# A feed-forward block on one NeuronCore: seven half-size products in place of eight

## What is computed

```python
D_MODEL = 1024
D_FF = 4 * D_MODEL

def _rmsnorm(x, g):
    xf = x.astype(jnp.float32)
    y = xf * lax.rsqrt(jnp.mean(xf * xf, axis=-1, keepdims=True) + NORM_EPS)
    return (y * g.astype(jnp.float32)).astype(x.dtype)

def _mlp(h, w1, w2):
    a = jax.nn.relu(jnp.einsum('btd,df->btf', h, w1))
    return jnp.einsum('btf,fd->btd', a * a, w2)
```

## Time and profile before

| what | value |
|---|---|
| median of 3 runs | 2421.88 us (2419.75 to 2430.71) |
| the profiled execution, its own time | 2421.98 us |
| its span | 2420.4 us |
| PE busy | 2147.9 us, 89% of the span, 14280 matmuls |
| DVE, ACT, POOL busy | 36%, 29%, 14% |
| DMA | 154.45 MB, mean 64 GB/s |

### The profile page before, as it was taken

The page is one execution under the profiler, slowest core; times in us unless marked ns, Lnnn a source line. Parts: engine busy times, 40 slices in busy tenths (PEclk is TensorE's granted clock), DMA queues, the critical chain, the costliest instruction groups (busy, mean ns, idle before and its releaser), DMA issues. The chain is left out here.

```text
span 2420.4 us, 37774 instructions
## 1 busy us (share of the span) xinstructions
PE 2147.9 (89%) x14280; PEld 1437.8 (59%) x14280; DVE 863.1 (36%) x1637; ACT 701.1 (29%) x1285; POOL 330.9 (14%) x245
## 2 busy tenths in 40 slices
PE   4889966798998989989499969896999999999998
PEld 2445634576776667655366646564566666666666
DVE  4211141554544445454633444524222221221223
ACT  5112221343443434424333224312110110211212
POOL 4200022300000000000101111101430420510410
PEclk7998978899999999989799989997999999999999
DMA  6421442111111111131110024421111111111111
GB/s 210 115 69 49 149 122 66 53 46 37 54 36 55 36 37 54 37 84 35 28 44 9 21 98 138 136 107 35 52 47 49 50 46 52 44 51 52 43 35 72
DMA packets 191808, 154.45 MB, mean 64 GB/s; under 512 B 9200, under 2 KB 178310, under 8 KB 191370
## 3 DMA queue, kind: packets, MB, share of 16 engines
q1 hardware_dynamic: 182250, 140.01, 19.0%
q0 software_dynamic: 4640, 10.60, 1.6%
q10 hardware_dynamic: 4800, 2.30, 0.3%
HBM read 125.71 MB, written 31.33 MB: 65 GB/s over the span
## 5 line engine op out<-in xcount | busy, mean ns | idle before, releaser
L426 PE MATMUL ps<-hH,wH 128*128 128x352 f16 x1536 | 319.2, 317 | 47.7 <-ACTq L399 27.8
L426 PE MATMUL ps<-hL,wH 128*128 128x352 f16 x1536 | 318.0, 317 | 0.0
L426 PE MATMUL ps<-hH,wL 128*128 128x352 f16 x1536 | 317.2, 316 | 0.0
L413 DVE SCALAR_TENSOR_TENSOR wL<-w,wH 128x1024 f16<-128x1024 f32 x98 | 120.0, 1225 | 324.4 <-ACT wH L406 310.3
L426 PEld LDWEIGHTS ps<-hH,wH 128*128 128x128 f16 x1536 | 151.7, 99 | 134.0 <-issue 49.2
L426 PE MATMUL ps<-mH,wH 128*128 128x352 f16 x960 | 196.4, 314 | 9.5 <-DVEq L399 8.1
L426 PEld LDWEIGHTS ps<-hL,wH 128*128 128x128 f16 x1536 | 152.3, 99 | 82.4
L426 PEld LDWEIGHTS ps<-hH,wL 128*128 128x128 f16 x1536 | 151.8, 99 | 81.7
L426 PE MATMUL ps<-mL,wH 128*128 128x352 f16 x960 | 196.4, 314 | 0.0
L426 PE MATMUL ps<-mH,wL 128*128 128x352 f16 x960 | 196.0, 313 | 0.0
L1252 ACT COPY oL<-ps 128x512 f32<-128x512 f32 (+7 forms) x256 | 103.0, 402 | 297.2 <-PE ps L1211 297.2
(11 more groups left out here) (411 smaller groups left out, 2910.3 us busy)
## 6 DMA issues: line engine op xcount, KB each, us to landing
w<-in_mlp_w SPq DMA_DIRECT2D x64, 512.0 KB, 4.0
w<-in_w_in SPq DMA_DIRECT2D x32, 512.0 KB, 3.9
gw<-in_w_in SPq DMA_DIRECT2D x26, 512.0 KB, 4.7
gates<-cmpT SPq DMA_DIRECT2D x24, 528.0 KB, 3.0
mgsg<-gates SPq DMA_DIRECT2D x24, 528.0 KB, 4.3
mgw<-in_w_branch SPq DMA_DIRECT2D x24, 256.0 KB, 2.8
xTd<-xT SPq DMA_DIRECT2D x1, 4224.0 KB, 13.8
xT<-xTd SPq DMA_DIRECT2D x1, 4224.0 KB, 13.7
```

Source lines behind the costliest of these rows:

```text
L413: self.k.nc.vector.scalar_tensor_tensor(self.k.wL[:, slot % 2, :, :], self.k.w32[:, slot, :, :], WS, self.k.wH[:, slot % 2, :, :], ALU.mul ...
L426: ins = nc.tensor.matmul(k.ps[:, 3 * parity + c, 0:CH], w[:, kt, :], x[:, kt, c * CH:(c + 1) * CH], start=(kt == 0 and x is inH and w is w ...
```

## The change

`Dense` and `norm` are replaced for this block alone, by the class `Wino` and by `norm_wino`; `mlp` is rewritten. All other stages stay as they were.

The 1056 tokens are cut into two halves of 528 (`HT`), the contraction of 1024 into two halves of 512, and two weight tiles side by side form a pair, so that a pair is a 2 x 2 product of blocks. Instead of eight half-size products (128 x 512 by 512 x 528) it makes seven, P1 to P7, of sums and differences of blocks (Strassen's scheme, in the order `ORDER`). The four block sums of the weights are made by VectorE; `s1` holds one, three are written over `w32`. Those of the input are T1 to T4. Each product splits its own weight block into high and low, in a ring of four. It has 24 matmuls of 264 columns and a PSUM slot of two banks, four slots in rotation. There are 32 pairs, 224 products.

What comes out of PSUM is joined by more block sums. ScalarE copies P1 (`one`) and P5 (`five`) out, and VectorE takes out the other five with an addition. In the first layer GpSimd joins two blocks, VectorE squares the four blocks in place with the ReLU, and since the second layer needs T1 to T4 of the squared activations too, GpSimd subtracts those four. All seven operands (B11, B21, B22, T1 to T4) are then split: high parts on ScalarE, low parts of B on VectorE, low parts of T on GpSimd. In the second layer GpSimd makes the six additions to `xT` that the seven products need beside VectorE's. At the start of `mlp` the block sums T2, T3 and T4 of the norm's output are made and split, in instructions of 4 x 528 columns.

```diff
+HT = T // 2
+HC = HT // 2
+PAIRS = 2 * FF // (2 * P)
+GROUP = 2 * KD // 2
+ORDER = ('P1', 'P2', 'P6', 'P7', 'P4', 'P5', 'P3')
...
 def norm_wino(k, gcol, nxt):
...
+            for kt in range(KD):
+                nc.vector.scalar_tensor_tensor(cols3(nxt.x[kt // 4][:, kt % 4, :]), cols3(xT[:, kt, :]), k.vec[:, gcol + kt:gcol + kt + 1],
+                                               dense_out(k.ps, 0), ALU.mult, ALU.mult).then_inc(scaled, 1)
+            dve.wait_ge(scaled, KD)
+            tt(nxt.spare[0], nxt.x[0][:, :, HT:T], nxt.x[0][:, :, 0:HT], ALU.subtract)
...
         @block.tensor
         def _(pe):
+                pe.wait_ge(wn.lo, rel(PER, p + 1))
...
+                for kt in range(4):
+                    if n % GROUP == FIRST and kt in (0, 2, 3):
+                        made = n - FIRST + max(kt, 1)
+                        if u[0] == 'B':
+                            pe.wait_ge(b_lo, rel(3 * FIRST, b_at(made, u)))
+                        else:
+                            pe.wait_ge(t_lo, rel(4 * FIRST, t_at(made, u)))
+                    for w, x in ((wH, xH), (wH, xL), (wL, xH)):
+                        for c in range(2):
+                            ins = nc.tensor.matmul(k.ps[:, 2 * (p % 4) + c, 0:HC], w[:, kt, :], x[:, kt, c * HC:(c + 1) * HC],
...
         @block.scalar
         def _(act):
+            for p, (n, q) in enumerate(seq):
+                for u in H_BEFORE.get(p, ()):
+                    h_high(u)
+                if p + 3 < N:
+                    split(p + 3)
+                if first_layer(n) and q == 'P6':
+                    a_high(n, 'B11')
+                if first_layer(n) and q == 'P5':
+                    a_high(n, 'B21')
+                if n and first_layer(n - 1):
+                    for u in {'P1': ('T2',), 'P2': ('B22', 'T3'), 'P7': ('T4', 'T1')}.get(q, ()):
+                        a_high(n - 1, u)
+                if n > PAIRS - FIRST and q in ('P2', 'P6'):
+                    square_x(n - 1, ('P2', 'P6').index(q))
+                if q in ('P1', 'P5'):
+                    copy_out(p, n, q)
...
         @block.vector
         def _(dve):
+            sums(0, ('P5', 'P7', 'P6'))
+            tt(hx['T2'], hx['B22'], hx['T1'], ALU.subtract).then_inc(h_made, 1)
+            split(2)
+            h_low('T2')
+            sums(0, ('P3',))
+            for p, (n, q) in enumerate(seq):
+                for u in H_BEFORE.get(p, ()):
+                    h_low(u)
+                if p + 3 < N:
+                    split(p + 3)
+                if q == 'P5' and n + 1 < PAIRS:
+                    sums(n + 1, ('P5', 'P7', 'P6'))
+                elif q == 'P1' and n:
+                    sums(n, ('P3',))
...
+                if n and first_layer(n - 1) and q == 'P6':
+                    b_low(n - 1, 'B22')
+                if q in ('P2', 'P6', 'P7', 'P4', 'P3'):
+                    out(p, n, q)
+                if first_layer(n):
+                    for u in {'P2': ('B11',), 'P4': ('B21',), 'P3': ('B12', 'B22')}.get(q, ()):
+                        square(n, u)
+                    for u in {'P6': ('B11',), 'P5': ('B21',)}.get(q, ()):
+                        b_low(n, u)
...
         @block.gpsimd
         def _(pool):
+            tt(hx['T3'], hx['B22'], hx['B12'], ALU.subtract).then_inc(h_shared, 1)
+            pool.wait_ge(h_made, 1)
+            tt(hx['T4'], hx['B21'], hx['T2'], ALU.subtract).then_inc(h_shared, 1)
...
+                if not first_layer(n):
...
+                    x_add(n, '11+1', one)
...
+                    x_add(n, '12+2', c12)
...
+                    x_add(n, '21+3', c22)
+                    x_add(n, '22+3', c22)
...
+                    x_add(n, '12+5', five)
+                    x_add(n, '22+5', five)
+                    continue
+                pool.wait_ge(copied, copied_at(n, 'P5'))
+                pool.wait_ge(evac, evac_at(n, 'P4'))
+                tt(c12, c12, five, ALU.add).then_inc(joined, 1)
+                tt(c22, c22, five, ALU.add).then_inc(joined, 1)
+                pool.wait_ge(joined, joined_at(n, 'B22'))
+                pool.wait_ge(squared, squared_at(n, 'B12'))
+                tt(five, c12, c11, ALU.subtract).then_inc(t_made, 1)
+                pool.wait_ge(squared, squared_at(n, 'B22'))
+                pool.wait_ge(t_made, t_made_at(n, 'T1'))
+                tt(t2, c22, five, ALU.subtract).then_inc(t_made, 1)
+                tt(t3, c22, c12, ALU.subtract).then_inc(t_made, 1)
+                t_low(n, 'T2')
+                t_low(n, 'T3')
+                pool.wait_ge(b_lo, b_at(n, 'B21'))
+                tt(c21, c21, t2, ALU.subtract).then_inc(t_made, 1)
+                t_low(n, 'T4')
+                t_low(n, 'T1')
```

More of the change, by code:

```diff
@@ new lines, in norm_wino, with part @@
+def norm_wino(k, gcol, nxt):
+    nc, xT = k.nc, k.xT
+    summed, ms_ready, root_ready, step = k.sem("n2_summed"), k.sem("n2_ms"), k.sem("n2_root"), k.sem("n2_step")
+    diag_ready, spread, scaled, hi_ready = k.sem("n2_diag"), k.sem("n2_spread"), k.sem("n2_scaled"), k.sem("n2_hi")
+    NC = NT + 1
+    with nc.sbuf_tensor("n2dg", [P, NC, P], F32) as diag, nc.sbuf_tensor("n2st", [P, 4, 16], F32) as st, nc.Block() as block:
+        ms, root, y, t2 = (st[:, i, 0:NC] for i in range(4))
+        def part(kt):
+            u = 'B11' if kt < 4 else 'B21'
+            return nxt.x[kt // 4][:, kt % 4, 0:HT], nxt.h[u][0][:, kt % 4, :], nxt.h[u][1][:, kt % 4, :]
@@ L2248, in _ @@
         @block.sync
         def _(sp):
[L2250 to L2259, removed]
+            for n in range(2):
+                for i in range(2):
+                    nxt.load(sp, n, i)
@@ L2261, in _ @@
         @block.tensor
         def _(pe):
[L2263 to L2273, removed]
+            for t in range(NC):
+                w = P if t < NT else TS
+                ins = nc.tensor.matmul(k.ps[0:w, 7, t:t + 1], k.ssq[:, t * P:t * P + w], k.c('ones')[:, 0:1], start=True, stop=True)
@@ L2275, in _ @@
+            ins.then_inc(summed, 1)
+            pe.wait_ge(diag_ready, 1)
+            for c in range(3):
+                ins = nc.tensor.matmul(k.ps[:, c, 0:CH], k.c('ones'), diag[:, :, :].rearrange("p t n -> p (t n)")[:, c * CH:(c + 1) * CH],
+                                       start=True, stop=True)
+            ins.then_inc(spread, 1)
         @block.scalar
         def _(act):
[L2277 to L2286, removed]
@@ L2288, in _ @@
-            dn.split_hi(act, 0, 0, 0)
-            groups(act, tile)
+            act.wait_ge(ms_ready, 3)
+            nc.scalar.activation(root, ms, ACT.Sqrt).then_inc(root_ready, 1)
+            nxt.wait_tile(act, 0, 1)
+            for p in range(2):
+                nc.scalar.activation(nxt.ring(p)[0], nxt.quarter(0, 1, p + 1), ACT.Copy, scale=WS).then_inc(nxt.hi, 1)
+            for kt in range(KD):
+                x, hi, lo = part(kt)
+                act.wait_ge(scaled, kt + 1)
+                nc.scalar.copy(hi, x).then_inc(hi_ready, 1)
@@ L2291, in _ @@
         @block.vector
         def _(dve):
[L2293 to L2306, removed]
@@ new lines, in _, with settle @@
+            dve.wait_ge(root_ready, 1)
+            made = [0]
+            def settle(ins):
+                made[0] += 1
+                ins.then_inc(step, 1)
+                dve.wait_ge(step, made[0])
+            settle(nc.vector.reciprocal(y, root))
+            settle(tt(t2, y, y, ALU.mult))
+            settle(tt(t2, t2, ms, ALU.mult))
+            settle(ts(t2, t2, -0.5, 1.5, ALU.mult, ALU.add))
+            settle(tt(y, y, t2, ALU.mult))
+            tt(diag[:, :, :], k.c('ident').unsqueeze(1).broadcast_to([P, NC, P]), y.unsqueeze(2).broadcast_to([P, NC, P]),
+               ALU.mult).then_inc(diag_ready, 1)
@@ L2313, in _ @@
         @block.gpsimd
         def _(pool):
[L2315 to L2323, removed]
-                    nc.gpsimd.tensor_tensor(aL[:, t, :], sq[:, :], aH[:, t, :], ALU.subtract).then_inc(lo_made, 1)
+            for kt in range(KD):
+                x, hi, lo = part(kt)
+                pool.wait_ge(hi_ready, kt + 1)
+                nc.gpsimd.tensor_tensor(lo, x, hi, ALU.subtract)
@@ L2487, in build @@
             k.end_stage()
-            mp = Dense(k, "mp", 2 * FF // P, ahead=[w_tile(d['mlp_w1'], i * P) for i in range(4)])
-            norm(k, "n2", VG2, mp)
+            mp = Wino(k, "mp")
+            norm_wino(k, VG2, mp)
             k.end_stage()
```

297 lines of the change are left out of this document (293 added, 4 removed).

## The result

| | before | after |
|---|---|---|
| median of 7 runs | 2422.5 us (2419.03 to 2430.71) | 2439.1 us (2436.54 to 2444.56) |
| after by before | | 1.0068, 95% interval 1.0053 to 1.0083 |
| profiled execution | 2421.98 us, span 2420.4 | 2436.67 us, span 2435.0 |
| the block, first matmul to last evacuation's end | 691.8 us | 711.4 us |

What follows compares the result with a forecast made beforehand. VectorE, held by GpSimd over SBUF, was to set first-layer pairs at 23.2 us, TensorE second-layer ones at 18.9. From 2421.98 us, norm -3.9, block -7.0 and end +1.0 gave 2412 us, range 2365 to 2445.

Steps and rivals of the forecast that it cites:

- The port: First layer: VectorE and GpSimd wait for each other over SBUF operands, costing VectorE 0.86 us (float32) or 0.98 (float16).
- The turn: Going to the second layer, TensorE waits some 5 us for T2's low part, then runs at low clock, taken as 2.5.
- The four second-layer parts: The four second-layer pairs of each group, set by TensorE, with the pause and low clock at their start: 78.0 us.
- The norm: Norm before the block: three VectorE low parts of 1.25 us go, one of 2.3 comes; block begins 3.9 us earlier.
- Float32 out: 1.947 at 1056, with the same fixed part 1.07.: GpSimd's float32 instructions in the block: 1.07 us each at 528 columns, scaled from 1.947 us at 1056.
- Its first pair carries no T work from before, and TensorE sets it: 18.9.: First-layer part of each later group: its first pair takes TensorE's 18.9 us, three more make 88.5.
- 3.7 on GpSimd: Block's start: GpSimd's instructions over 2112 columns take 3.7 us each; the first pair ends at 37.7 us.
- That costs TensorE 1.7 us of its 4.3 us of slack: First-layer pairs: after TensorE's longest pause, 2.3 us ahead of P3, half clock costs 1.7 us, nothing on the path.
- Rival 2: VectorE slower, waits between instructions and no overlap of starts: 26.1 us a first-layer pair, 2447 us; chance 0.13.
- rival 1: Conflicts of VectorE and GpSimd cost little, less than 3.9 us a pair: all pairs 18.9 us, 2345 us; chance 0.20.
- rival 3: Weight loads set TensorE's pace, 0.125 us a matmul: a pair takes 21.0 us, kernel 2452 us; chance 0.03.
- rival 4: Pauses keep TensorE at half clock half of the time in the first layer: 58 us more, 2470 us; chance 0.06.

Runs made afterwards that it cites:

- the run with the same tensor twice: Changed kernel, but GpSimd's six float32 instructions of a first-layer pair read one tensor twice and add it: 2417.6 us, 0.9971 of before.
- the memsets: Changed kernel, but from the second group on GpSimd's ten first-layer instructions are memsets of 1296 columns, which read nothing: 2390.0 us, block 650.8 us.

## Why the prediction was wrong

**What held.** TensorE's pace: steady second-layer pairs take 18.9 us, 0.1125 us a matmul. The prediction's estimate of 23.1 us a pair, worked out from the 128-column figure of the Trainium skill, "TensorE: Matmul & The Clock Gate", section "Back-to-back issue gap", is not borne out: 25 ns more on each matmul do not come at 264 columns. The section states no sustained figure for that width. The port: who waits for whom, that it goes either way, that evacuations are free. VectorE's own prices, 0.69 and 0.70 us, and GpSimd's float16 one, 1.18 us alone at 528 columns. The turn: P6 stands 5.3 us until T2's low part (forecast 5.0), and the clock falls behind it, in the second group as these windows show (TensorE at rest in the first, granted 0.50 in the next):

```profile
1978.30:1981.70 3.40, 0.00 (x0) 0.00 (x0) 2.77 (x2) 1.15 (x3) 3.26 (x3) 1.00 0.00 0
1981.70:1985.10 3.40, 1.68 (x8) 1.20 (x9) 2.86 (x3) 2.23 (x5) 3.40 (x4) 0.50 0.01 4
```

The four second-layer parts came within 1.1 us each. The norm (-4.2 for -3.9) and the squares at the end (+1.2 for +1.0) held too.

**What failed**, by the steps:
- "Float32 out: 1.947 at 1056, with the same fixed part 1.07." It measures 1.30 us, and costs VectorE 1.08 us where the two alternate (1.16 + 0.55 - 0.63) for 0.86. Steady pairs 23.96 for 23.2, +9.1 us in all, and part of each later group's first pair; in the run with the same tensor twice the block is 24 us shorter, 17 of them in the steady pairs. This step decides the sign by the runs: with the assumed duration the kernel is at 0.9971 of before, with the pauses of the next step gone it is still at 1.0041. The mechanism was right and its size was taken from the wrong row: L2321 was the only GpSimd float32 instruction of that width there, but it reads one tensor, and the prediction set no upper bound beside it.
- "Its first pair carries no T work from before, and TensorE sets it: 18.9." Counted from evacuation to evacuation it takes 22.6 to 24.8: 1.7 to 2.2 beyond the usual step are the pause at TensorE's jump (with 1.7 more at half clock in the fourth group), which the sum left out though the loop stands in the code; about 2 are P3's evacuation, which begins 2.4 us behind the start of TensorE's last matmul (1901.36 to 1903.74) and not 0.3 (1880.72 to 1881.04), since VectorE has a low part of 1.81 and one of 1.78 us ahead of it, each held by one of the two joins. +13.4 us, the largest error in the table.
- "3.7 on GpSimd" for 2112 columns: 5.03 us, the same error as the first (twice 1.3 more). P6 of the first pair waited 9.2 us for 6.2; the first pair 39.8 for 37.7, +2.1.
- "That costs TensorE 1.7 us of its 4.3 us of slack": in the steady pairs TensorE stands 5.0 us, the longest time 1.9 us ahead of P4 and not ahead of P3, and the clock does not fall in them. As slack it was nothing on the path either way.
- The final norm, 1.8 us longer, had no term; it runs at a granted clock of 0.81 and moves 159 GB/s of output, and what lengthened it was not tried.

+26.5 in the block, +1.8 behind it, -0.1 in norm and end, and -3.8 from the stages before: 2412.1 becomes 2436.5, the profiled execution's 2436.67 to 0.2.

**The rivals.** Rival 2 had the outcome, slower, but not the way to it. By its own threshold, 24.0 us a pair "where the change is no gain", the steady pairs of 23.96 make the change even; what made it slower than that are the first pairs of the groups and the start, which rival 2 does not have. Nor was its reason, no overlap of starts, the right one: VectorE's independent starts overlap by 0.07 us (1757.26 + 1.79 against 1758.98), and what made the pair longer lies on GpSimd. The conflicts are not small (rival 1): the memsets show what they cost, 711.4 less 650.8 with only three groups of four freed, some 60 us, turns included. Weight loads (rival 3) set no pace. The clock (rival 4) falls at each turn, and else only in the first pair and behind the third jump.
